# Weighted sum of gathered expert rows: multiply-adds on VectorE against products with diagonal matrices on TensorE

## What is computed

```python
def chunk_fn(args):
    xc, ic, gc = args
    h = jax.nn.gelu(jnp.einsum('td,thkd->thk', xc, u_tab[ic]), approximate=False)
    return jnp.einsum('thk,thkd->td', gc * h, v_tab[ic])
...
x = x + peer_ffn(rmsnorm(x, ffn_norm_w[i]), ...)
gate = jax.nn.sigmoid(rmsnorm(x, ple_norm_w[i]) @ ple_w_gate[i])
x = x + gate * (p[i] @ ple_w_proj[i])
```

## Time and profile before

| | us |
|---|---|
| median of 3 runs | 3561.73 (3560.79 to 3563.55) |
| span of the profiled execution, the only time known of it | 3562.6 |
| DVE busy | 2243.2 (63%) |
| PE busy | 1836.8 (52%) |
| POOL busy | 1171.6 (33%) |
| ACT busy | 841.8 (24%) |

### The profile page before, as it was taken

How to read it: one execution, slowest core, us unless ns; L and a number is a source line. 1 busy time by engine, 2 the same in 40 slices (tenths; PEclk the granted TensorE clock), 3 DMA queues, 4 the chain that set the end, 5 groups by cost and what they waited for, 6 DMA issues and landing times.

```text
span 3562.6 us, 29832 instructions
## 1 busy us (share of the span) xinstructions
PE 1836.8 (52%) x10624; PEld 1615.9 (45%) x10624; DVE 2243.2 (63%) x2463; ACT 841.8 (24%) x1210; POOL 1171.6 (33%) x648
## 2 busy tenths in 40 slices
PE   5999889999999889866888000000000000000029
PEld 5888779888998778744678000000000000000027
DVE  3444445444544444333356988888888888888874
ACT  3444444433444343122343000000000000000023
POOL 0000000000000000000000288888888888888820
PEclk9999999999999999855799555555555555555569
DMA  5444445455545454400242489999999999999963
GB/s 173 164 147 151 142 146 183 165 196 192 178 165 190 165 183 145 112 0 12 95 156 92 162 344 385 383 375 388 387 378 386 383 386 385 392 377 385 380 269 124
DMA packets 234640, 839.18 MB, mean 236 GB/s; under 512 B 21692, under 2 KB 29196, under 8 KB 168253
## 3 DMA queue, kind: packets, MB, share of 16 engines
q0 software_dynamic: 73728, 536.90, 38.0%
q1 hardware_dynamic: 154188, 298.44, 25.1%
q10 hardware_dynamic: 6640, 2.70, 0.3%
HBM read 835.86 MB, written 2.13 MB: 235 GB/s over the span
## 4 chain that ended last, share of the span: by engine, by line
PE 49%; POOL 27%; issue 11%; DVE 9%; ACT 2%; DMA 1%; ACTq 1%; POOLq 0%; DVEq 0%
POOL vrows L1567 13%; POOL big L1560 10%; PE bank L1231 8%; PE bank L1233 8%; PE bank L1234 8%; PE bank L1251 6%; PE bank L1255 6%; PE bank L1253 6%; POOL idxc L1551 4%; DMA big<-in_peer_u,idxc 1%; PE bank L1459 1%; PE bank L1480 1%; PE bank L1262 1%; DVE eacc L1178 1%; DVE Al L744 1%
## 5 line engine op out<-in xcount | busy, mean ns | idle before, releaser
L754 DVE TENSOR_TENSOR wl<-raw,wh 128x1024 fp32r<-128x1024 f32 (+1 forms) x544 | 654.4, 1210 | 826.2 <-ACT wh L466 826.1
L1262 PE MATMUL bank<-cst,big 128*128 128x128 f32 x61 | 12.4, 375 | 1515.9 <-DMA big<-in_p 1494.8
L466 ACT CAST wh<-raw 128x1024 fp32r<-128x1024 f32 (+1 forms) x544 | 561.7, 1038 | 883.8 <-PE bank L1234 512.2
L1262 PEld LDWEIGHTS bank<-cst,big 128*128 128x128 f32 x61 | 10.4, 195 | 1516.9 <-DMA big<-in_p 1495.0
L1165 DVE CUSTOM_DVE_ANT_0 big<-big,tmp 128x2048 f32<-128x2048 f32 x256 | 576.7, 2291 | 185.9 <-DMA big<-in_peer_u,idxc 171.9
L1178 DVE SCALAR_TENSOR_TENSOR eacc<-vrows,wcur,eacc 128x2048 f32<-128x2048 f32 x256 | 603.0, 2355 | 9.1
L1560 POOL DMA_INDIRECT big<-in_peer_u,idxc x256 | 514.0, 2008 | 172.6 <-POOL idxc L1551 101.1
L1567 POOL DMA_INDIRECT vrows<-in_peer_v,idxc x256 | 501.8, 1960 | 79.0 <-issue 77.4
L1251 PE MATMUL bank<-Ah,wh 128*128 128x256 f32 x1792 | 510.8, 285 | 8.1 <-DVE Al L744 8.1
L1253 PE MATMUL bank<-Al,wh 128*128 128x256 f32 x1792 | 509.8, 284 | 0.0
L1255 PE MATMUL bank<-Ah,wl 128*128 128x256 f32 x1792 | 509.7, 284 | 0.0
(11 more groups left out here) (202 smaller groups left out, 2188.4 us busy)
## 6 DMA issues: line engine op xcount, KB each, us to landing
raw<-in_mlp_w SPq DMA_DIRECT2D x128, 1024.0 KB, 5.1
raw<-in_sb_w_qkv SPq DMA_DIRECT2D x48, 1024.0 KB, 5.2
raw<-in_w_in SPq DMA_DIRECT2D x28, 1024.0 KB, 5.0
raw<-in_sb_w_o SPq DMA_DIRECT2D x16, 1024.0 KB, 5.1
raw<-in_w_out SPq DMA_DIRECT2D x16, 1024.0 KB, 5.1
raw<-in_peer_w_q SPq DMA_DIRECT2D x16, 1024.0 KB, 5.0
raw<-in_ple_w_gate SPq DMA_DIRECT2D x16, 1024.0 KB, 5.1
big<-in_peer_u,idxc POOLq DMA_INDIRECT x256, 8.8
```

Source lines behind the costliest of these rows:

```text
L466: nc.scalar.copy(whv[hq % 4][:, :, 0:width], raw_half[hq][:, :, 0:width]).then_inc(hi_done, 1)
L754: V_.tensor_tensor(wlv[hq % 4][:, :, 0:width], raw_half[hq][:, :, 0:width], whf[hq % 4][:, :, 0:width], ALU.subtract).then_inc(split_done, 1)
```

## The change

DVE no longer multiplies and adds the v rows. For each slot it writes a diagonal 128 x 128 matrix with the tokens' weights (the identity times the column of `wcur`) into `diag`, which lies where `accx` lay. PE multiplies this matrix with the slot's v rows, 4 products of 128 x 512, and sums them in PSUM: half 0 in banks 0 to 3, half 1 in banks 4 to 7. The first products into the banks are identity times x_res, so that the banks end with the new x_res, which DVE copies back. `v_done[g]` is now raised by PE, and the memset of the sum is gone.

```diff
-        accx = v3(eacc, 0, MT, D)
+        diag = [[eacc[:, (g * EG + b) * P:(g * EG + b + 1) * P] for b in range(EG)] for g in range(GROUPS)]
...
-            dve.wait_ge(acc_zero, 1)
...
-                    def adds(g):
+                    def weights(g):
                         dve.wait_ge(gelu_done[g], m * per + 1 + i)
                         V_.tensor_tensor(wcur[:, g * EG:(g + 1) * EG], hgel[:, g * EG:(g + 1) * EG],
                                          gts[:, bass.ds(i * (GROUPS * EG) + (m * SLOTS + g * EG), EG)], ALU.mult
                                          ).then_inc(w_done, 1)
                         dve.wait_ge(w_done, GROUPS * m * per + g + 1 + i * GROUPS)
-                        dve.wait_ge(v_landed[g], 16 * EG * (m * per + 1) + i * (16 * EG))
+                        dve.wait_ge(v_done[g], EG * m * per + EG + i * EG)
                         for b in range(EG):
-                            V_.scalar_tensor_tensor(accx[:, m, :], vbuf[g][b], wcur[:, g * EG + b:g * EG + b + 1],
-                                                    accx[:, m, :], ALU.mult, ALU.add).then_inc(v_done[g], 1)
-                            dve.wait_ge(v_done[g], EG * m * per + EG + b + 1 + i * EG)
+                            V_.tensor_scalar(diag[g][b], ident, wcur[:, g * EG + b:g * EG + b + 1], None, ALU.mult
+                                             ).then_inc(diag_ready[g], 1)
...
-                V_.tensor_tensor(xr[:, m, :], xr[:, m, :], accx[:, m, :], ALU.add).then_inc(peer_added, 1)
+                dve.wait_ge(v_done[GROUPS - 1], EG * (m + 1) * per + EG)
+                for n in range(NT):
+                    last = V_.tensor_copy(xr[:, m, n * 512:n * 512 + 512], banks[4 * m + n][:, :])
+                last.then_inc(peer_added, 1)
...
+            def sum_rows(m, i, last=False):
+
+                for g in range(GROUPS):
+                    pe.wait_ge(v_landed[g], 16 * EG * (m * per + 1) + i * (16 * EG))
+                    for b in range(EG):
+                        pe.wait_ge(diag_ready[g], EG * m * per + b + 1 + i * EG)
+                        for n in range(NT):
+                            mm = nc.tensor.matmul(banks[4 * m + n][:, :], diag[g][b], vbuf[g][b][:, n * 512:n * 512 + 512],
+                                                  start=False, stop=last and g == GROUPS - 1 and b == EG - 1)
+                        mm.then_inc(v_done[g], 1)
+
+            per = SLOTS // (GROUPS * EG)
+            wait_aux_evac(pe, X["psc"] + 7)
+            wait_acc_evac(pe, A_WQ + 2)
+            wait_acc_evac(pe, A_WQ + 3)
+            for m in range(MT):
+                for n in range(NT):
+                    nc.tensor.matmul(banks[4 * m + n][:, :], ident, xr[:, m, n * 512:n * 512 + 512], start=True, stop=False)
+                with pe.Fori(0, per - 1) as i:
+                    sum_rows(m, i)
+                sum_rows(m, per - 1, last=True)
+            pe.wait_ge(peer_added, 2)
...
-            nc.gpsimd.memset(accx, 0.0).then_inc(acc_zero, 1)
```

More of the change, by code:

```diff
@@ L296, in build @@
         idx_ready = sem("idx_ready")
-        acc_zero = sem("acc_zero")
+        diag_ready = [sem(f"diag_ready{g}") for g in range(GROUPS)]
         idx_copied = sem("idx_copied")
@@ L1184, in _ @@
                         dots(g)
-                        adds(g - 1)
-                    adds(GROUPS - 1)
-                V_.tensor_tensor(xr[:, m, :], xr[:, m, :], accx[:, m, :], ALU.add).then_inc(peer_added, 1)
+                        weights(g - 1)
+                    weights(GROUPS - 1)
+                dve.wait_ge(v_done[GROUPS - 1], EG * (m + 1) * per + EG)
+                for n in range(NT):
+                    last = V_.tensor_copy(xr[:, m, n * 512:n * 512 + 512], banks[4 * m + n][:, :])
+                last.then_inc(peer_added, 1)
             rms(5)
```

## The result

| | before | after |
|---|---|---|
| median, us | 3561.26 | 3451.64 (3449.76 to 3454.68) |
| ratio after / before | | 0.9691 (95%: 0.9677 to 0.9704) |
| span of the profiled execution | 3562.6 | 3447.9 |
| DVE busy | 2243.2 | 1703.9 |
| PE busy | 1836.8 | 2853.1 |

The changed kernel is 110 us faster; 97 were forecast. Busy time of 1000 us in the loop, with the granted clock, the DMA share and the rate last, answers to the earlier trace rows; the line for 2300 to 3300 us is followed by POOL's groups, which answer to the earlier trace rows, and the gather queue (packets, MB, share), which answers to the earlier trace rows.

A forecast was written before the change was run, and what follows sets the result against it. The prediction took POOL's gather issues, held by DVE instructions, to bound the loop. Transfers -110, start +5, middle +2 and end +6 summed to -97 us on 3562.6, giving 3465 us; range 3438 to 3545, the forecast's own 3440 to 3500.

The forecast's parts named there:

- POOL sets the pace, and DVE sets POOL's: Gather loop: POOL never waits for a buffer and needs 10.95 us per group, 5.2 of them held by DVE instructions.
- The rule against the row: Gather issues: the skill's rule, as read, says DVE's adds don't hold them; the trace shows 2.1 us against 0.95.
- rival A: Gather loop: the queue gets no fuller, POOL keeps 10.95 us per group; +11 us, 3573 us; chance 0.08.
- The transfers: Gather loop: transfers set the pace at 417 GB/s, 10.06 us per group instead of 10.95; -110 us (-142 to -44).
- The start: Start of the gather loop: PE starts cold, so the first v_done comes later; +5 us (+3 to +9).
- The middle: Between the token halves: DVE waits for PE's last group and copies four banks; nine us of cover, +2 us (0 to +8).
- The end: From the last u rows to finished x_res: 21 to 23 us instead of 17; +6 us (+4 to +12).
- Sum: Whole kernel: -110 + 5 + 2 + 6 = -97 us on a span of 3562.6, giving 3465 us.
- PE's clock: PE products in the loop: 6.9 us per group at full clock, 8.7 starting at half clock; hidden beside transfers of 10.06.
- Rival B: PE in the loop: clock stays at half, 13.7 us per group, PE becomes the bound; +368 us, 3930 us; chance 0.07.
- A': Gather loop: transfers gain only the missing 3%, 10.59 us per group; -31 us, 3531 us; chance 0.15.
- C: Gather loop: the queue runs at 428 GB/s or above; -129 us, 3433 us; chance 0.05.

The follow-up runs named there:

- a1: Changed kernel plus two unneeded DVE multiply-adds of 128x2048 per group, both inputs in SBUF; 3602 us, ratio 1.011 to the kernel before.
- a2: Changed kernel plus two unneeded DVE reductions of 128x2048 per group, one input in SBUF; 3449 us, ratio 0.968 to the kernel before.
- a3: Changed kernel plus four unneeded DVE scalings of 128x2048 per group, one SBUF input at double pace; 3507 us, ratio 0.985 to the kernel before.
- c2: Changed kernel with ten instead of eight PE products of 128x512 per group; 3457 us, ratio 0.971 to the kernel before.
- c3: Changed kernel with twelve instead of eight PE products of 128x512 per group; 3518 us, ratio 0.988 to the kernel before.
- b2: Kernel before with DVE's multiply-adds kept but accumulating in PSUM, four of 128x512 per slot, without PE; 3497 us, ratio 0.982.

## Why the prediction was right

**POOL sets the pace, and DVE sets POOL's.** Right, and now shown by a1 and a2: the same load on DVE costs 150 us in one form and nothing in the other. What the prediction didn't see is the form. It wrote that each POOL instruction is held until "a DVE instruction" ends. It is an instruction with two inputs in SBUF, or one at double pace; one with a single input passes. The trace before held a hint, though a weak one: gathers ahead of the loop were issued while DVE was busy 23.6 of 24 us, and were hardly held (0.94 to 1.19 us). But DVE's instructions there last 0.4 us at most, so that even one that holds POOL shows little.

**The rule against the row.** The prediction set the Trainium skill, "SBUF — State Buffer", section "Who interferes with whom", against the trace, and there it misread the rule. The section says that a VectorE instruction with two SBUF inputs contends with a GpSimd instruction that reads SBUF, that one in a 2-port mode contends with GpSimd, and that one with at most one SBUF input outside these modes does not. Only of the writing of descriptors does it infer that two inputs leave it alone. A gather issue also reads: its indices come from `idxc` in SBUF. So by the rule it is held, and the runs agree: 2.0 to 2.1 us beside two inputs in a1, 1.8 to 2.0 beside the double pace in a3, 0.94 beside the one-input reductions in a2. The inference isn't contradicted either: the issue at 2721.53 ended at 2723.70, so its last 0.8 us ran beside the second multiply-add, and the two together took 4.74 us, hardly more than 2 x 2.35. That what is held is the reading of the indices is my reading; no run changes how the issue gets them. The price of the hold, 5.2 us per group, the prediction took from rows, and rival A, whose result that reading of the rule would give, is out: the issues fell to 1.1 us.

**The transfers.** The term was 10.95 to 10.06 us per group, -110 us; the queue ran at 422 GB/s, 9.94 us. From the first to the last index copy it is 3281.28 - 2061.64 = 1219.6 us against 1347.3, **-128 us**, and the transfers' gap of the middle is in it. The rate was taken as the middle of 419 and 414; the full queue gave slightly more than the better one. By the rate it would be (10.95 - 9.94) x 123 = 124 less the 4.6 of the middle; the other 8 us are, as I read it, a queue that is deeper at the end than at the start, so that POOL's copies run ahead of the landings. The trace bears that out: between the two copies the transfers moved 419 GB/s x 1219.6 us = 511 MB, and 123 groups are 516 MB.

**The start.** Forecast +5. The first index copy came at 2061.64 instead of 2053.96, +7.7, but 2.1 of it had arisen before (POOL's issues behind the router began at 2042.58 instead of 2040.43), so +5.5. PE started at the half clock, as costed.

**The middle.** Forecast +2, with a cover of nine us. The cover was not enough:

```profile
2680.56 2.48 DVE L1187 COPY x_res<-bank 128x512 f32<-128x512 f32 x4 [14.93 <-PE bank L1527]
...
2692.47 21.90 PE L1527 MATMUL bank<-vrows,eacc 128*128 128x512 f32 x47 [8.51 <-DVE eacc L1177]
...
2701.26 0.78 POOL L1573 COPY idxc<-gbc 128x2 uint32 x1 [12.97 <-PE bank L1527]
...
2700.00:2712.00 12.00, 12.00 (x29) 5.32 (x28) 5.32 (x10) 0.20 (x1) 7.88 (x8) 1.00 0.72 261
```

DVE waited 15 us for PE's last group, did four dots before the first weights of the second half, PE then started at the half clock, and POOL got its first buffer 13 us late. For 12 us the rate was 261 GB/s: (422 - 261) / 422 x 12 = **4.6 us** lost, inside the bounds of 0 to 8. The step that fell short is that more delays add up here than were added: the forecast counted PE's pair of groups and the copies (17 us), but not the two pairs of dots behind them and the burst at the half clock.

**The end.** Forecast +6. From the last u rows to x_res it is 3323.9 - 3300.7 = 23.2 us against 17: **+6.3**.

**Sum.** -127.7 + 7.7 + 6.3, and 0.5 between the last copy and the last u rows, are -113 us up to x_res; the span fell by 114.7. The profiled execution lies 3.7 us below the median, and the medians differ by 110.

**PE's clock.** Rival B is out: mean granted clock 0.90 in the loop. In the stretches of the burst of 9.48 us above, with the columns as before:

```profile
2605.36:2607.50 2.14, 2.14 (x3) 1.11 (x4) 0.30 (x1) 0.00 (x0) 1.53 (x3) 0.50 0.98 410
2607.50:2610.00 2.50, 2.50 (x4) 0.95 (x4) 0.00 (x0) 0.00 (x0) 1.56 (x2) 0.50 1.03 429
2610.00:2614.00 4.00, 4.00 (x10) 1.83 (x10) 3.77 (x3) 0.00 (x0) 0.00 (x0) 0.99 1.00 418
```

After a pause of 4.2 us the first 4.6 us ran at the half clock. This group took 9.5 us, not the 8.7 of the forecast, still under the transfers' 9.94, but with little room. That the forecast held doesn't rest on this room: in c2 and c3, with shorter pauses, the clock was at 0.98 and 1.00.

**The other rivals.** A' (the queue gains only the missing 3%) and C (428 GB/s) missed on either side of 422.

## What to carry to other kernels

Where POOL issues gathers one after the other, look at the order in time for issues that end just behind DVE instructions, and ask for each long DVE instruction beside them how many of its inputs lie in SBUF and whether it runs at double pace: the form of the instruction can be worth more than its length. A transfer share of 97% is not a full queue; compare the rate with a stretch in which many transfers are outstanding. When work moves to an engine that was idle, its steady cost may be nothing, but price each place where the pipeline is drained (start, middle, end), and there add the delays up.

## What the runs showed of the hardware

The DMA share does not tell how near a queue is to its best. At a share of 1.00 the rate was 403 GB/s in a3, 407 in b2 and 408 in c3, where a group took 10.3 to 10.4 us, and 422 at 1.01 where gathers were always queued; before the change it was 384 at 0.97. A packet seems to take longer when few are queued behind it, but no run isolates that.

The f32 products of 128x512 with a diagonal matrix ran at 0.43 us per record, the same as the same shape in the earlier trace rows, and DVE's dots kept their 2.29 us beside them.
